# Half-width block inversion of a delta-rule mixer, its masked copies moved to GpSimd, and its norms moved to a later stage

## The chip, the cores and the metric

The program runs on one core of one Trainium2 chip. The metric is the device time of one execution in microseconds (us). The engines are named as in the profile: PE (TensorE, with PEld for its weight loads), DVE (VectorE), ACT (ScalarE), POOL (GpSimd) and SP (SyncE, which issues the DMAs).

## What is computed

The reference is two small transformer stacks in float32, one after the other, on 256 tokens of width 1024. The first has a block with an mLSTM and stick-breaking mixer, then a block with a gated delta-rule mixer; each block ends in a cross-attention on a memory of 256 tokens and a squared-ReLU feed-forward. The second has a block with two kinds of attention and one with a block attention, each followed by a gated feed-forward. The change touches the delta-rule mixer, which solves one unit lower triangular system for each head and chunk:

```
def gated_deltanet(q, k, v, beta, log_alpha):
...
    kk = jnp.einsum('nbhtd,nbhsd->nbhts', kc, kc)
    lower = jnp.where(strict, bc[..., :, None] * kk * decay, 0.0)
    eye = jnp.eye(L, dtype=f32)
    rhs = jnp.concatenate([vc * bc[..., None], kc * (bc * jnp.exp(g))[..., None]], axis=-1)
    sol = lax.linalg.triangular_solve(lower + eye, rhs, left_side=True, lower=True, unit_diagonal=True)
...
    _, o = lax.scan(step, S0, (u_c, w_c, attn, q_dec, k_dec, g_last))
    return _from_chunks(o)
```

The result of each head is normed over its 128 values and multiplied by a gain and by the SiLU of a gate. The kernel uses two chunks of 128 tokens in place of the reference's chunks of 64, which gives the same result.

## The kernel before

The weights are streamed from HBM as 458 panels of 128 x 1024 float32 (8 blocks of 128 x 128 each), in a fixed order, into a ring of six slots (`RING`). SP fetches panel n as soon as PE has counted panel n - 6 as used (L305 to L312). ACT rounds each panel to `ring_hi` (`reach`, L910 to L917), up to `LEAD` = 3 panels ahead of the stage that it serves, and POOL makes `ring_lo`, the rest, in two pieces of 128x512 for each panel (`low_part`, L321 to L327); `ring_lo` lies over the raw panel. The activations are split in the same way (`x_hi`, `x_lo`), and `project` and `project_tokens` (L379 and L421) form hi*hi + lo*hi + hi*lo on PE. All engines run their own instruction streams, written out in order in Python, and meet by semaphores. A `bank` of PSUM is taken in turn from four of ACT and four of DVE, and PE waits for what frees it.

The delta-rule stage of the first stack has eight heads, in two halves of four (`for half in range(2)`, PE L720, ACT L1157, DVE L1679). One half has eight 128 x 128 matrices: four heads by two chunks, in two groups `g` of four, each group one PSUM bank. In a half:

1. For each head, PE broadcasts the gate row (`gb`), DVE and ACT form the decays, PE the key and query products, and DVE writes `gd_at` (the strictly triangular matrix, transposed) and `gd_attn` (L1684 to L1699).
2. The inversion runs over seven levels (`LEVELS`). At level k, `cut(k, g)` (DVE, L1702) multiplies `gd_at` by a 0/1 mask that keeps the blocks that join neighbouring diagonal blocks of size 2^k, and writes `gd_b`. PE forms Y = B^T T (4 matmuls a group, ACT copies Y to `gd_y`), then the update of T (`gd_t`, not at the last level) and that of its transpose (`gd_tt`), 4 matmuls each; DVE subtracts them (`renew`, L1708). The matmuls are float32, and each one is two records in the trace.
3. A chain of small products for the four heads ends in the head outputs in `qkv4[:, 2]` and their squares in `sq`; two matmuls with a matrix of ones sum the squares (PE L796 to L798), and ACT computes the inverse root twice (`rsqrt`, L1200).

`mix_heads(0)` (DVE, L1671) takes these factors of the first half, norms the heads and multiplies by the gate; it stands in DVE's stream of the second half, after the first head of step 1 (L1681). ACT computes the SiLU of the whole gate (128x2048) in the first half, between steps 1 and 2 (L1181), with a table load before and after it.

After the second half, `memory_side` (PE L547, ACT L997) projects the memory into keys (four banks of two output tiles each, `xk1`) and values (four banks, `xv1`), 16 panels in all; DVE forms the memory's parts first (`mem_parts`), then `mix_heads(1)` and `mix_parts`, from which the mixer's output projection starts. POOL's stream holds nothing but `low_part`, in one loop over the ring (L329 to L334), so that it does nothing while no panel is used. Through the whole delta-rule stage no panel is used: the ring is full and all queues stand.

Of the kernel before, what the change touches and what calls it, by code (L numbers as in the profile page):

```python
# [45 lines left out]
P = 128  # L46
T = 256
# [85 lines left out]
def build_program(nc, panels, consts_in, smalls_in, x_in, mem_in, pos_in, out):  # L133
    with ExitStack() as ctx:
# [106 lines left out]
        gd_cols = area(16384, 8, 8)  # L241
        gd_row = lambda i: mixT[0:GD_H, (4 + i) % C, :]
# [77 lines left out]
        def _(pool):  # L320
# [8 lines left out]
            rounds = N_PANELS // RING  # L329
            with pool.Fori(0, rounds) as r:  # L330
                for s in range(RING):
                    low_part(s, r * RING + s)
            for n in range(rounds * RING, N_PANELS):
                low_part(n % RING, n)  # L334
# [7 lines left out]
        def _(pe):  # L342
# [377 lines left out]
            for half in range(2):  # L720
# [21 lines left out]
                for k in range(LEVELS):  # L742
                    y_at = {}
                    for g in range(2):
# [6 lines left out]
                        else:  # L751
                            o = bank("act", "y_ready")
                            for j in range(4):
                                mm(o[:, j * P:(j + 1) * P], gd_b[:, 4 * g + j, :], gd_t[:, 4 * g + j, :], True, True,
                                   "act" if j == 3 else None)
                            y_at[g] = told.seen["y_ready"]
                    for g in range(2 if k else 0):
                        pe.wait_ge(sem("y_ready"), y_at[g])
                        pe.wait_ge(sem("t_ready"), t_at[g])
                        if k < LEVELS - 1:  # L760
                            o = bank("dve", "t_ready")
                            for j in range(4):
                                mm(o[:, j * P:(j + 1) * P], gd_tt[:, 4 * g + j, :], gd_y[:, 4 * g + j, :], True, True,
                                   "dve" if j == 3 else None)
                        o = bank("dve", "t_ready")
                        for j in range(4):
                            mm(o[:, j * P:(j + 1) * P], gd_y[:, 4 * g + j, :], gd_tt[:, 4 * g + j, :], True, True,
# [120 lines left out]
        def _(act):  # L888
# [268 lines left out]
            for half in range(2):  # L1157
# [21 lines left out]
                if half == 0:  # L1179
                    settle()  # L1180
                    tell(act.activation(gate, gate, ACT.Silu), "gate_silu")  # L1181
                    log_exp()
# [10 lines left out]
                for hh in range(HALF):  # L1193
# [3 lines left out]
                    tell(act.activation(sq[:, 4 + hh, :], o[:, 0:T], ACT.Square), "osq")  # L1197
                if half:
                    told.more("mixed", 2)
                for g in range(2):  # L1200
                    rsqrt(2 * T, 1.0 / P)
            memory_side(1, 0, 4)
# [71 lines left out]
        def _(dve):  # L1274
# [395 lines left out]
            levels = const("levels_t").rearrange("p (k c) -> p k c", c=P)  # L1670
# [8 lines left out]
            for half in range(2):  # L1679
                for s in range(HALF + 1):  # L1680
                    if half and s == 2:  # L1681
                        told.more("gate_silu")
                        mix_heads(0)
# [18 lines left out]
                def cut(k, g):  # L1702

                    settle()
                    tell(dve.tensor_tensor(gd_b[:, 4 * g:4 * g + 4, :], gd_at[:, 4 * g:4 * g + 4, :],  # L1705
                                      spread(levels[:, k, :], 4), ALU.mult), "b_ready")

                def renew(m, g):  # L1708
                    o = take().rearrange("p (j b) -> p j b", b=P)
                    m = m[:, 4 * g:4 * g + 4, :]  # L1710
                    tell(dve.tensor_tensor(m, m, o, ALU.subtract), "t_ready")  # L1711

                for g in range(2):
                    cut(0, g)
                for g in range(2):
# [5 lines left out]
                    cut(1, g)  # L1721
                for k in range(1, LEVELS):
                    for g in range(2):
                        if k < LEVELS - 1:
                            renew(gd_t, g)
                            cut(k + 1, g)
# [222 lines left out]
```

## Time and profile before

| what | us |
| --- | --- |
| median of 3 runs | 1736.66 (1736.13 to 1749.96) |
| the profiled execution's own time | 1722.62 |
| its span | 1720.8 |
| busy in it: PE | 1603.2 (93%) |
| PE weight loads | 1514.6 (88%) |
| DVE | 796.1 (46%) |
| ACT | 808.1 (47%) |
| POOL | 1188.0 (69%) |

The span is what the profiler saw of one execution; the execution itself took 1.8 us more. The busy shares are means over the whole span, so they tell little of one stage: for that, the rows further down are taken from stretches of the trace, with their times counted from the start of the span. "PEclk" is the granted TensorE clock as a share of full speed. A row of a timeline gives the start, the duration of the merged instructions, their engine, line and operation, and in square brackets how long the engine sat idle before them and what ended that.

### The profile page before, as it was taken

To read this page: it belongs to the slowest core of one execution; us is meant where nothing else is said; L and a number is where in the kernel's file an instruction comes from. 1 tells how busy PE (TensorE), PEld (TensorE's weight loads), DVE (VectorE), ACT (ScalarE), POOL (GpSimd) and SP (SyncE) were. 2 spreads that over 40 slices of the span, in tenths; PEclk is the share of its full clock that TensorE was granted. 3 is DMA by queue.
4 is the path that set the end of the run, shared out by engine and by line. 5 is a ranking of instruction groups with operands and counts; after the bars stand their busy time and mean duration, and the time that the engine had idled before them with its cause. 6 is when DMAs were issued, how large, how long until landed. Compare 5 with 4: busy or idle time off the path is not lost.

```text
span 1720.8 us, 32818 instructions
## 1 busy us (share of the span) xinstructions
PE 1603.2 (93%) x12776; PEld 1514.6 (88%) x12776; DVE 796.1 (46%) x1430; ACT 808.1 (47%) x1169; POOL 1188.0 (69%) x920
## 2 busy tenths in 40 slices
PE   4979999999999987999999996989999999899997
PEld 3976998999988785999999995978999999799997
DVE  6038366320166465636532004655655335575523
ACT  3473544554455435444455442555555443644442
POOL 3733994899967600098589993653899988279995
PEclk7998999999999998999999998999999999999999
DMA  5421553565544300055355552432566654155552
GB/s 213 160 88 63 172 181 111 172 196 192 191 157 154 116 1 1 13 173 181 110 173 191 193 195 72 136 111 84 175 196 195 193 168 143 58 169 193 195 196 98
DMA packets 67086, 248.55 MB, mean 144 GB/s; under 512 B 7440, under 2 KB 7696, under 8 KB 66448
## 3 DMA queue, kind: packets, MB, share of 16 engines
q1 hardware_dynamic: 66960, 246.69, 43.8%
q8 instruction: 101, 1.65, 0.4%
q14 instruction: 25, 0.20, 0.0%
HBM read 245.62 MB, written 1.05 MB: 143 GB/s over the span
## 4 chain that ended last, share of the span: by engine, by line
PE 52%; DVE 7%; ACT 1%; issue 1%; DVEq 0%; ACTq 0%
PE ps_dve L361 42%; PE ps_act L361 10%; DVE x_lo L1378 1%; DVE x_hi L1375 1%; PE ps_act L372 1%; DVE xT L1370 1%; DVE work L1711 1%; ACT work L977 1%; DVE work L1409 0%; DVE sq L1363 0%; DVE work L1705 0%; ACT work L931 0%; DVE sq L1343 0%; DVE xT L1328 0%; DVE x_lo L1335 0%
## 5 line engine op out<-in xcount | busy, mean ns | idle before, releaser
L326 POOL TENSOR_TENSOR ring_lo<-ring,ring_hi 128x512 fp32r<-128x512 f32 x916 | 1187.8, 1335 | 511.5 <-ACT ring_hi L917 508.5
L917 ACT ACTIVATE ring_hi<-ring 128x1024 fp32r<-128x1024 f32 x458 | 465.8, 1052 | 193.3 <-DMA ring<-panels 190.9
L361 PE MATMUL ps_dve<-x_hi,ring_hi 128*128 128x256 f32 x1728 | 415.6, 281 | 17.6 <-DVE x_lo L1378 17.4
L361 PE MATMUL ps_dve<-x_lo,ring_hi 128*128 128x256 f32 x1728 | 412.9, 279 | 0.0
L361 PEld LDWEIGHTS ps_dve<-x_hi,ring_hi 128*128 128x128 f32 x1728 | 328.8, 190 | 23.2 <-DVE x_lo L1378 18.9
L361 PEld LDWEIGHTS ps_dve<-x_lo,ring_hi 128*128 128x128 f32 x1728 | 329.1, 190 | 0.2
L361 PE MATMUL ps_dve<-x_hi,ring_lo 128*128 128x256 f32 x1728 | 243.1, 278 | 0.0
L361 PE MATMUL ps_dve<-work_parts,ring_hi 128*128 128x256 f32 x1728 | 225.3, 276 | 0.0
L361 PEld LDWEIGHTS ps_dve<-x_hi,ring_lo 128*128 128x128 f32 x1728 | 219.1, 190 | 0.2 <-POOL ring_lo L326 0.2
L361 PEld LDWEIGHTS ps_dve<-work_parts,ring_hi 128*128 128x128 f32 x1728 | 211.8, 188 | 0.0
L1370 DVE TENSOR_TENSOR xT<-xT,ps_dve 128x512 f32<-128x512 f32 x40 | 27.5, 688 | 325.7 <-PE ps_dve L361 325.1
L361 PE MATMUL ps_dve<-work 128*128 128x128 f32 (+4 forms) x800 | 122.5, 325 | 13.4 <-DVE scratch L1688 5.7
L361 PE MATMUL ps_dve<-work_parts,ring_lo 128*128 128x256 f32 x864 | 132.7, 276 | 0.0
L361 PEld LDWEIGHTS ps_dve<-work 128*128 128x128 f32 (+1 forms) x800 | 101.0, 203 | 34.7 <-issue 19.8
L931 ACT ACTIVATE work<-ps_act 128x512 f32<-128x512 f32 (+2 forms) x122 | 64.4, 528 | 141.4 <-PE ps_act L361 136.1
L361 PE MATMUL ps_act<-x_hi,ring_hi 128*128 128x256 f32 x392 | 101.5, 296 | 24.6 <-DVE x_lo L1335 16.5
L361 PEld LDWEIGHTS ps_dve<-work_parts,ring_lo 128*128 128x128 f32 x864 | 113.8, 188 | 0.0
L361 PEld LDWEIGHTS ps_act<-x_hi,ring_hi 128*128 128x128 f32 x392 | 77.3, 197 | 28.6 <-DVE x_lo L1335 18.6
L939 ACT ACTIVATE sq<-xT 128x512 f32<-128x512 f32 x40 | 25.3, 633 | 158.1 <-DVE xT L1370 158.1
L361 PE MATMUL ps_act<-x_lo,ring_hi 128*128 128x256 f32 x392 | 97.9, 287 | 0.0
L361 PE MATMUL ps_dve<-mix_hi,ring_hi 128*128 128x256 f32 x384 | 93.3, 280 | 0.0
L361 PE MATMUL ps_dve<-mix_lo,ring_hi 128*128 128x256 f32 x384 | 92.5, 278 | 0.0
(232 smaller groups left out, 2199.0 us busy)
## 6 DMA issues: line engine op xcount, KB each, us to landing
ring<-panels SPq DMA_DIRECT2D x458, 512.0 KB, 3.4
consts<-constants SPq DMA_DIRECT2D x1, 2208.0 KB, 14.8
xT<-x_t SPq DMA_DIRECT2D x1, 1024.0 KB, 5.0
memn<-mem_t SPq DMA_DIRECT2D x1, 1024.0 KB, 18.9
out_t<-xT SPq DMA_DIRECT2D x1, 1024.0 KB, 3.9
smalls<-small_operands SPq DMA_DIRECT2D x1, 849.5 KB, 7.9
consts<-constants SPq DMA_DIRECT2D x1, 129.5 KB, 4.8
angle_i<-positions SPq DMA_DIRECT2D x1, 128.0 KB, 6.3
```

The source lines that it names most:

```text
L326: pool.tensor_tensor(ring_lo[:, s, cs], ring[:, s, cs], plain(ring_hi[:, s, cs]), ALU.subtract).then_inc(sem("lo_made"), 1)
L361: ins = pe.matmul(o, lhsT, rhs, start=start, stop=stop, skip_group_check=True)
L372: mark(pe.transpose(o, a, ident[0:a.shape[0], 0:a.shape[0]]), full)
L917: tell(act.activation(ring_hi[:, n % RING, :], ring[:, n % RING, :], ACT.Copy), "hi_made")
L931: tell(act.activation(dst, src, func, scale=scale), name)
L939: tell(act.activation(sq[:, c:c + 2, :], xT[:, c:c + 2, :], ACT.Square), "to_add" if c < 2 * added else "squared")
L977: ins = act.activation(b[:, n, 0:cols], b[:, n, 0:cols], ACT.Exp, bias=pair_max[s % 3][:, 4 + n:5 + n])
L1370: tell(dve.tensor_tensor(xT[:, c:c + 2, :], xT[:, c:c + 2, :], o, ALU.add), "resid")
L1375: ins = dve.tensor_scalar(x_hi[:, i, :], xT[:, i, :], gain[:, i:i + 1], None, ALU.mult)
L1378: ins = dve.scalar_tensor_tensor(x_lo[:, i, :], xT[:, i, :], gain[:, i:i + 1], plain(x_hi[:, i, :]), ALU.mult, ALU.subtract)
L1711: tell(dve.tensor_tensor(m, m, o, ALU.subtract), "t_ready")
```

## The change

Four things change together:

- The masked copies are made by POOL (`cut` in its stream, between two calls of `low_parts`: the panel loop is split at panel `FIRST["xk1"] + LEAD + 1`). For a level above 1 a copy waits for `y_ready` of the level before, which frees `gd_b`.
- Only half of the columns is computed at each level: B^T T for the even blocks of columns (`even`), the update of T likewise, and that of its transpose for the odd blocks. Matmuls have 64 columns in place of 128, `renew` and the copy of Y 256 elements in place of 512, and ACT writes zeros to the other half of `gd_y` with a second instruction.
- The norms of both halves move into `memory_side`: two sums of squares behind its bank 1, two behind bank 2. DVE does both `mix_heads` after `mem_parts`.
- ACT's SiLU of the gate is cut in four pieces of 128x512, behind levels 1 to 4 of the first half.

```diff
+            ahead = FIRST["xk1"] + LEAD + 1
+            low_parts(0, ahead)
+            for half in range(2):
+                told.more("attn", HALF)
+                if half:
+                    told.more("osq", HALF)
+                for g in range(2):
+                    cut(0, g)
+                for k in range(1, LEVELS):
+                    for g in range(2):
+                        pool.wait_ge(sem("t_ready" if k == 1 else "y_ready"),
...
+                        cut(k, g)
+            low_parts(ahead, N_PANELS)
...
+                            pe.wait_ge(sem("t_ready"), t_at[g] - (k > 1))
                             o = bank("act", "y_ready")
                             for j in range(4):
-                                mm(o[:, j * P:(j + 1) * P], gd_b[:, 4 * g + j, :], gd_t[:, 4 * g + j, :], True, True,
+                                js = slice(4 * g + j, 4 * g + j + 1)
+                                mm(o[:, j * 64:(j + 1) * 64], gd_b[:, 4 * g + j, :], even(gd_t[:, js, :], k), True, True,
                                    "act" if j == 3 else None)
...
-                for g in range(2):
-                    pe.wait_ge(sem("osq"), told.seen["osq"] - 2 + 2 * g)
-                    mm(bank("act", "norm_used"), ones, sq[:, 4 + 2 * g:6 + 2 * g, :], True, True, "act")
-                if half:
-                    memory_side()
+
+            def delta_norms(i):
+                for g in {1: (0, 1), 2: (2, 3)}.get(i, ()):
+                    pe.wait_ge(sem("osq"), osq_at + 2 * g + 2)
+                    mm(bank("act", "norm_used"), ones, sq[:, 2 * g:2 * g + 2, :], True, True, "act")
+            osq_at = told.seen["osq"] - GD_H
+            memory_side(delta_norms)
...
-                        copy_out(gd_y[:, 4 * g:4 * g + 4, :], name="y_ready")
+                        y = gd_y[:, 4 * g:4 * g + 4, :]
+                        act.activation(even(y, k), dense(take(), k), ACT.Copy)
+                        tell(act.activation(odd(y, k), dense(const("ones"), k), ACT.Copy, scale=0.0), "y_ready")
+                    if half == 0 and k <= 4:
+                        gs = gate[:, 2 * k - 2:2 * k, :]
+                        tell(act.activation(gs, gs, ACT.Silu), "gate_silu")
+                log_exp()
...
+            memory_side(1, 0, 2)
+            for g in range(4):
+                if g == 2:
+                    memory_side(1, 2, 3)
+                if g >= 2:
+                    told.more("mixed")
+                rsqrt(2 * T, 1.0 / P)
+            memory_side(1, 3, 4)
...
-                    if half and s == 2:
-                        told.more("gate_silu")
-                        mix_heads(0)
...
             mem_parts()
+            told.more("gate_silu", 4)
+            mix_heads(0)
             mix_heads(1)
```

The order of instructions on DVE, at the start of the second half. In the kernel before, from the first head's last product to the second head's (`work` holds the matrices, `rstd` the norm factors, `scratch` the decays):

```order
L1699 TENSOR_TENSOR work<-ps_dve,scratch 128x256
L1312 SCALAR_TENSOR_TENSOR ps_act<-ps_act,rstd 128x512 [waits rstd,attn,gate_silu]
L1313 SCALAR_TENSOR_TENSOR ps_act<-ps_act,rstd 128x512 [waits dve_step]
L1315 SCALAR_TENSOR_TENSOR rstd<-ps_act,rstd 128x512 [waits dve_step]
L1676 SCALAR_TENSOR_TENSOR work<-work,smalls,rstd 128x512 [waits norm_used]
L1677 TENSOR_TENSOR mixT<-work 128x512 [waits dve_step]
```

The same place in the changed kernel, up to the next head's first instruction:

```order
L1745 TENSOR_TENSOR work<-work,scratch 128x128
L1746 TENSOR_TENSOR work<-ps_dve,scratch 128x256
L1734 COPY scratch<-ps_dve 128x512 [waits dve_full,attn]
L1735 TENSOR_TENSOR scratch<-ps_dve,consts 128x256
L1742 TENSOR_TENSOR work<-ps_dve,scratch 128x256 [waits decays,dve_full,gb]
```

The five instructions of `mix_heads` (twice over, ten in all) are gone from between the heads; they stand behind `mem_parts` now.

ACT's order in the memory's key projection, before: `hi` copies of panels (L917), copies of the finished banks (L931), and one wait for `mixed` behind the last key bank.

```order
L931 ACTIVATE work<-ps_act 128x512 [waits act_full,hi_made]
L917 ACTIVATE ring_hi<-ring 128x1024 [waits panel_here1]
L917 ACTIVATE ring_hi<-ring 128x1024 [waits panel_here2]
L931 ACTIVATE work<-ps_act 128x512 [waits act_full,hi_made]
L917 ACTIVATE ring_hi<-ring 128x1024 [waits panel_here3,mixed]
```

The same place in the changed kernel, from the copy of bank 2 on (L963 makes `hi`, L977 copies a bank, L990 to L999 are one `rsqrt`):

```order
L977 ACTIVATE work<-ps_act 128x512 [waits act_full,hi_made]
L990 ACT_TABLE_LOAD [waits mixed]
L998 ACTIVATE rstd<-ps_act,consts 128x512 [waits act_full,mem_keys]
L999 ACTIVATE rstd<-rstd 128x512 [waits act_step]
L990 ACT_TABLE_LOAD [waits mixed]
L998 ACTIVATE rstd<-ps_act,consts 128x512 [waits act_full,rstd]
L999 ACTIVATE rstd<-rstd 128x512 [waits act_step]
L963 ACTIVATE ring_hi<-ring 128x1024 [waits panel_here1]
L963 ACTIVATE ring_hi<-ring 128x1024 [waits panel_here2]
L977 ACTIVATE work<-ps_act 128x512 [waits act_full,hi_made]
L963 ACTIVATE ring_hi<-ring 128x1024 [waits panel_here3,mixed]
```

Two `rsqrt`, each behind a wait for a `mixed` of DVE, stand between the copy of key bank 2 and the next `hi` copies of panels.

## Rows read from the trace of the kernel before

**Rows 1.** Timeline of PE in the inversion (first half; the last row, second half)

```profile
607.75 4.18 PE L361 MATMUL ps_act<-work 128*128 128x128 f32 x16 [1.48 <-DVE work L1705]
...
616.12 1.06 PE L361 MATMUL ps_act<-work 128*128 128x128 f32 x8
617.35 1.16 PE L361 MATMUL ps_act<-work 128*128 128x128 f32 x8 [0.17 <-DVE work L1705]
618.34 3.74 PE L361 MATMUL ps_dve<-work 128*128 128x128 f32 x32
621.92 1.06 PE L361 MATMUL ps_act<-work 128*128 128x128 f32 x8
...
687.61 2.26 PE L361 MATMUL ps_act<-work 128*128 128x128 f32 x16
```

**Rows 2.** Stretches: length; busy us of PE, PEld, DVE, ACT, POOL; clock, DMA, GB/s

```profile
607.00:613.00 6.00, 5.22 (x22) 4.92 (x23) 2.67 (x4) 3.39 (x4) 0.00 (x0) 0.50 0.02 4
620.00:630.00 10.00, 9.65 (x84) 9.28 (x83) 7.77 (x12) 1.79 (x3) 0.00 (x0) 1.00 0.00 0
1480.00:1500.00 20.00, 18.82 (x158) 15.73 (x155) 12.07 (x56) 14.64 (x36) 0.00 (x0) 1.00 0.00 1
```

**Rows 3.** Timeline of DVE around both starts of a half

```profile
592.55 0.69 DVE L1687 COPY scratch<-ps_dve 128x512 f32<-128x512 f32 x1
...
603.61 0.42 DVE L1699 TENSOR_TENSOR work<-ps_dve,scratch 128x256 f32<-128x256 f32 x1
...
655.45 0.69 DVE L1687 COPY scratch<-ps_dve 128x512 f32<-128x512 f32 x1 [11.05 <-PE ps_dve L361]
...
674.48 0.42 DVE L1699 TENSOR_TENSOR work<-ps_dve,scratch 128x256 f32<-128x256 f32 x1
```

**Rows 4.** Timeline of PE at the end of the first half and of the second

```profile
652.13 2.16 PE L361 MATMUL ps_act<-sq,consts 128*128 128x512 f32 x4
654.22 1.98 PE L361 MATMUL ps_dve<-mixT,consts 8*128 8x512 f32 x4
...
723.50 2.16 PE L361 MATMUL ps_act<-sq,consts 128*128 128x512 f32 x4
725.09 0.68 PE L361 MATMUL ps_act<-x_hi,ring_hi 128*128 128x256 f32 x1
```

**Rows 5.** Timeline of PE: float32 matmuls with 4 and 65 moving columns

```profile
1075.71 3.73 PE L361 MATMUL ps_dve<-smalls,sq 128*128 128x4 f32 x32
...
1161.09 1.45 PE L361 MATMUL ps_dve<-work 128*128 128x65 f32 x12
```

**Rows 6.** Timeline of ACT: copy of Y, copies of 256 elements, `rsqrt`, key banks

```profile
617.27 0.60 ACT L931 ACTIVATE work<-ps_act 128x512 f32<-128x512 f32 x1 [4.65 <-PE ps_act L361]
...
650.38 0.38 ACT L1196 ACTIVATE work<-ps_act 128x256 f32<-128x256 f32 x1 [0.39 <-PE ps_act L361]
650.66 0.38 ACT L1197 ACTIVATE sq<-ps_act 128x256 f32<-128x256 f32 x1
...
724.49 1.28 ACT L944 ACT_TABLE_LOAD   x1
...
727.16 1.28 ACT L944 ACT_TABLE_LOAD   x1
...
737.06 0.60 ACT L931 ACTIVATE work<-ps_act 128x512 f32<-128x512 f32 x1 [3.16 <-PE ps_act L361]
...
742.71 0.60 ACT L931 ACTIVATE work<-ps_act 128x512 f32<-128x512 f32 x1 [3.16 <-PE ps_act L361]
```

**Rows 7.** Lines by themselves: shortest, median and longest duration in ns

```profile
L1370 DVE TENSOR_TENSOR xT<-xT,ps_dve x40: 686/687/691, 215.8 to 1707.2; 128x512 f32<-128x512 f32 x40
...
L1677 DVE TENSOR_TENSOR mixT<-work x4: 691/692/1662, 664.0 to 734.0; 128x512 f32<-128x512 f32 x4
```

**Rows 8.** Timeline of POOL before the mixer, and from the memory stage on

```profile
459.37 18.87 POOL L326 TENSOR_TENSOR ring_lo<-ring,ring_hi 128x512 fp32r<-128x512 f32 x15
...
730.84 33.66 POOL L326 TENSOR_TENSOR ring_lo<-ring,ring_hi 128x512 fp32r<-128x512 f32 x24 [141.66 <-ACT ring_hi L917]
```

More of the change, by code:

```diff
@@ L327, in low_part, with low_parts, cut @@
                                        ALU.subtract).then_inc(sem("lo_made"), 1)
[L329 to L334, printed above, removed]
+            def low_parts(start, stop):
+                n = start
+                while n < stop and n % RING:
+                    low_part(n % RING, n)
+                    n += 1
+                rounds = (stop - n) // RING
+                if rounds:
+                    with pool.Fori(n // RING, n // RING + rounds) as r:
+                        for s in range(RING):
+                            low_part(s, r * RING + s)
+                for n in range(n + rounds * RING, stop):
+                    low_part(n % RING, n)
+            told = Counts(pool, sem)
+            levels = const("levels_t").rearrange("p (k c) -> p k c", c=P)
+            def cut(k, g):
+                mask = levels[:, k:k + 1, :].broadcast_to((P, 4, P))
+                pool.tensor_tensor(gd_b[:, 4 * g:4 * g + 4, :], gd_at[:, 4 * g:4 * g + 4, :], mask,
+                                   ALU.mult).then_inc(sem("b_ready"), 1)
+            ahead = FIRST["xk1"] + LEAD + 1
[9 more added lines that the diff above has]
+                        pool.wait_ge(sem("t_ready" if k == 1 else "y_ready"),
+                                     half * (2 + 2 * (2 * (LEVELS - 2) + 1)) + g + 1 if k == 1 else half * 2 * (LEVELS - 1) + 2 * (k - 2) + g + 1)
+                        cut(k, g)
+            low_parts(ahead, N_PANELS)
         hidden_from = {}
@@ L1178, in _ @@
                         tell(ins, "act_out")
[L1179 to L1182, printed above, removed]
                 for k in range(1, LEVELS):
                     for g in range(2):
-                        copy_out(gd_y[:, 4 * g:4 * g + 4, :], name="y_ready")
+                        y = gd_y[:, 4 * g:4 * g + 4, :]
[5 more added lines that the diff above has]
+                log_exp()
                 for hh in range(HALF):
@@ L1196, in _ @@
                     act.activation(qkv4[:, 2, h, :], o[:, 0:T], ACT.Copy)
[L1197 to L1202, printed above, removed]
+                    tell(act.activation(sq[:, h, :], o[:, 0:T], ACT.Square), "osq")
+            memory_side(1, 0, 2)
[6 more added lines that the diff above has]
+            memory_side(1, 3, 4)
             squares("c_out", C, 4)
@@ L1700, in _, with renew @@
                 dve.wait_ge(sem("attn"), half * HALF + HALF)
[L1702 to L1714, printed above, removed]
+                def renew(m, k):
+                    tell(dve.tensor_tensor(m, m, dense(take(), k), ALU.subtract), "t_ready")
                 for g in range(2):
@@ L1724, in _ @@
                         if k < LEVELS - 1:
-                            renew(gd_t, g)
-                            cut(k + 1, g)
-                        renew(gd_tt, g)
+                            renew(even(gd_t[:, 4 * g:4 * g + 4, :], k), k)
+                        renew(odd(gd_tt[:, 4 * g:4 * g + 4, :], k), k)
             mem_parts()
+            told.more("gate_silu", 4)
+            mix_heads(0)
             mix_heads(1)
```

16 lines of the change are left out of this document (11 added, 5 removed).

## The prediction, made before the changed kernel was run

> **What bounds the kernel now.** I read three views. The page's rows by slice show PE near full nearly everywhere, and a stretch in the middle where POOL and the DMA queues stand: POOL is idle for 141.66 us before its row at 730.84 [rows 8]. That is the delta-rule stage; nothing streams there, so a microsecond saved in it is one off the end, as long as the stages behind it, which are bound by PE, do not give it back. The timeline of PE shows what one level of the inversion costs: its first group starts at 616.12 and that of the next level at 621.92, 5.80 us later [rows 1]. In it stand 8 + 8 + 32 = 48 matmul records; the 32 take 3.74 us with the tail of the last one, and the next row starts 3.58 us after them, 0.112 us each. 48 of these are 5.4 us: PE is the bound of a level, and only about 0.35 us is waiting, on DVE's masked copy (0.17 us idle before 617.35 in PE's row) and around it. The table of stretches agrees: 9.65 of 10 us busy, clock 1.00, POOL 0.00 [rows 2].
>
> **Does half the width halve PE's time?** The rows say no. A float32 matmul with 65 moving columns and full weights comes 12 times in 1.45 us, and one with 4 columns 32 times in 3.73 us [rows 5]; less a tail of some 0.15 us that is 0.11 us a record, the same as with 128 columns. So it is the weights, 128 columns each time, that set the pace, and their number stays 48 a level. I cost the narrower matmuls at 0.113 us, no gain.
>
> The Trainium skill speaks on both sides here. "TensorE: Matmul & The Clock Gate", section "Back-to-back issue gap", gives a gap that falls with the moving columns (about 25 to 30 ns at 64); by that, doubled for the passes of float32, a record would need half of 0.11, which is the first rival below. The section on LDWEIGHTS in the same page lets the load go by the weight's columns, 107 ns for 128; this trace agrees with the latter (0.11 us at 4, 65 and 128 columns).
>
> **The change part by part**, against the span of 1720.8 us.
>
> *Levels 2 to 6.* ACT copies Y to two places: a PSUM copy of 256 elements starts 0.28 us before its successor and lasts 0.38 [rows 6], so the pair ends 0.66 us after its start, against 0.60 now; ACT starts 1.15 us after the group's first record (616.12 to 617.27) [rows 1, 6]. Y of group 0 is ready 1.81 us in, where PE's 16 records of the Ys also end (16 x 0.113), so about 0.1 us of waiting. The copies on POOL: the nearest row is its subtract of the same size, 15 in 18.87 us, 1.26 us each; the 24 from 730.84 on take 1.40 each [rows 8]. Two per level, started 1.9 and 3.2 us in, are there at 3.3 and 4.6, and PE wants them at 5.5 and 6.4. They are hidden by PE's 32 records; without that cover they would add up to 2 x 1.26. `renew` shrinks from 0.69 to about 0.42 us and is hidden anyway. A level becomes 5.55: 4 intervals a half x 0.25 = 1.0, and about 0.3 at the last `renew`, which PE awaits. For both halves -2.6.
>
> *The start of an inversion.* Here POOL is on the path. The first cut of each group, then the build of T on DVE (L1719, L1720), then the second cut stand in a row. First half: `attn` is complete at 603.61 + 0.42 = 604.03 [rows 3]; the cut ends at 605.4, DVE's build at 607.8, the second cut at 609.2, where PE has its first Y at 607.75 now [rows 1]. L1719 has two SBUF operands. Such a row, L1677, takes 0.69 us alone and 1.66 us beside POOL, while L1370, with one operand in PSUM, stays at 0.686 to 0.691 through all of its 40 calls [rows 7]; so I charge L1719 up to 0.97 us more and `renew` nothing. Group 1's Y then starts at 611.5, and the next level at 611.5 + 5 x 8 x 0.113 = 616.0, against 616.12 now. That it is not later is due to the clock: in 607 to 613 it stands at 0.50 [rows 2] (1.2 GHz; PE had been mostly idle before), and the first 16 records take 4.18 us with their gap [rows 1]. With 64 columns I keep 0.113 us at that clock too. The bounds are 0.113 and the 0.21 that 128 columns cost there; I take the lower, because at full clock nothing of the columns showed, and keep 3.5 us a half for the other end. Second half: `attn` at 674.90, the next level at 687.61, 12.7 us now; as the first half, 12.0. Together -0.8.
>
> The skill's page "SBUF — State Buffer" (the shared port pair) has DVE and GpSimd lock each other out for a whole instruction. By that rule the wait could be a full 1.26 us, 0.3 more per L1719; it would make the four of them 1.2 us dearer. The trace, with 0.97, is a little below it.
>
> *Between the halves.* Today PE does two sums of squares from 652.13, the next broadcast at 654.22 [rows 4], and DVE starts 1.23 us later at 655.45 [rows 3]. It then needs until 674.90, 19.45 us, because the ten instructions of `mix_heads(0)` stand between the heads; in the first half the same work took 592.55 to 604.03, 11.5 us. Now the broadcast goes at 652.1, DVE at 653.4, and it is done at 664.9: -10.0. ACT's two `rsqrt`, 2.67 us each [rows 6], leave too. Its `log_exp` load of 1.28 us behind level 6 falls into the time of PE's last 16 records and costs nothing. The four pieces of SiLU (about 0.6 us each, one load) fall into ACT's pauses, 4.65 us before the copy at 617.27; nothing.
>
> *The end of the second half.* The sums of squares leave from before the memory stage: 725.09 - 723.50 = -1.6 [rows 4].
>
> *The memory stage.* They come back here: 4 x 1.0 = +4.0, since PE is the bound (5.65 us a bank, 737.06 to 742.71) [rows 6]. And new waits come. With 0 at its start: bank 1 is done at 11.3, the sums at 13.3; ACT's two `rsqrt` give factors at 15.2 and 17.8. DVE needs for each of four parts 3 x 0.70 + 0.75 + 1.66 + gaps = 4.7 us beside POOL, so `norm_used` of the second comes at 22.1 and frees the bank of key bank 3, where PE has been ready since 20.9: 1.2 us. ACT waits for `mixed` (24.6) before its fourth `rsqrt`, which ends at 27.3; only then does it make `hi` of panels 9 and 10, so PE's value bank 0 starts 0.5 late (28.4 for 27.9) and waits about 0.8 on POOL's low part of panel 9. Then ACT waits for the last `mixed` at 34.0, and panel 11 is late by 0.3 and its low part by 0.8. Sum 3.6 us of stalls. POOL, at 1.40 us a piece just as fast as PE's 2.82 us a panel, loses its lead: +0.5. `mix_parts` ends at 46.7, before the output projection at about 53. Bounds of the stalls: 0, and 8 if the lead is not won back. Memory stage: +8.1.
>
> Sum: -2.6 - 0.8 - 10.0 - 1.6 + 8.1 = -6.9 us, a span of 1713.9. The profiled execution's own time would be 1715.7; the median of the runs shown lies 14.0 above that of before (1736.66 against 1722.62), so I predict 1729.8 as the median, 0.4% less.
>
> **The rivals.**
> 1. *Half width pays in full.* Then PE needs 24 x 0.113 = 2.7 us a level and the bound becomes the chain Y, copy, update, `renew`, with POOL's two copies: about 3.6 us. 10 intervals x 1.95 = 20 us more, and some 2 at the last levels: -29, 1708. For it: cycles fed to the array do halve. Against it: rows 5. Chance 0.10.
> 2. *The moved norms cost no stall*, since DVE is quicker than I have it (L1676 and L1677 not slowed), and the second half keeps its full clock: -6.9 - 4.1 - 2 = -13, 1724; its better half lies beyond 1%. Chance 0.22.
> 3. *The clock stays down (slower).* At 64 columns the array works half of the time, and if that does not lift the clock to 2.4 GHz, all 272 narrow records of a half run at it; it costs from the point at which a record needs over 0.13 us. At 0.21, the price of 128 columns there, 2 x 272 x 0.10 = +54, less the 6.9: +47, 1784. Against it: in 1480 to 1500, with many 65-column records, the clock is 1.00 [rows 2], and 4 columns for 3.7 us ran at 0.11 us. Chance 0.07.
> 4. *POOL does not keep up*, so the change does not do what it says: a copy with a repeated mask operand takes over 2.3 us; at 2.5 each level is about 0.7 longer, 10 x 0.95 = +9.5 against 5.55, +3 in all, 1740. Against it: all POOL rows of this size. Chance 0.07.
>
> **How the numbers follow.** My forecast has 0.54; its own range, from the bounds of the half-clock price (+7) and the stalls (-3.6 to +4.4), is 1724 to 1741. About 1% is what a measurement of this kernel can tell from no change, 17 us. Faster by more: rival 1 (0.10), half of rival 2 (0.11) and 0.03 of my own, 0.24. Slower by more: rival 3 (0.07) and 0.01. Within: 0.68. The range for 8 in 10 leaves out rival 3 and the better part of rival 1: 1710 to 1745.
>
> **What would show it.** PE's rows in the inversion: 48 records in some 5.4 us with 128x64 (right), or 2.7 (rival 1), or the clock at 0.50 beyond the first level (rival 3). POOL's copies near 1.26 us and no idle time of PE named after them from level 2 on. DVE without `mix_heads` between the heads, and 11.5 us from broadcast to last `attn`. PE's idle time in the memory stage, named after DVE (`norm_used`), ACT's `hi` and POOL's low part, 3 to 4 us. If a level is far from 5.55 or the memory stage from 53, I am wrong there.

## The result: slower by 2.8%, and the trace after

The changed kernel takes 1786.04 us (median, 1780.59 to 1800.19), beside 1743.31 us of the kernel before on the same chip: a ratio of 1.0279, interval 1.0232 to 1.0327 (the two medians alone give 1.0245, inside it). I had 1729.8 and a range up to 1745. The profiled execution took 1780.59 us; its span is 58.0 us longer than that of before (1778.8 against 1720.8).

The page of the changed kernel, its first two parts (busy time, then 40 slices of 44 us in tenths):

```profile
span 1778.8 us, 32742 instructions
PE 1661.7 (93%) x12776; PEld 1574.2 (89%) x12776; DVE 767.9 (43%) x1402; ACT 812.0 (46%) x1197; POOL 1224.0 (69%) x948
PE   4979999999999898999999998898999999899997
PEclk7998999999999757599999999898999999999999
```

PE looks as busy as ever. The row under it is the one to read: in slices 14 to 17, which are the delta-rule stage, the granted clock is 0.7, 0.5, 0.7, 0.5. The timeline of PE in the first inversion shows what one level costs now; it answers to [rows 1]:

```profile
614.71 1.97 PE L401 MATMUL ps_act<-work 128*128 128x64 f32 x8 [1.83 <-POOL work L358]
617.20 1.97 PE L401 MATMUL ps_act<-work 128*128 128x64 f32 x8 [0.53 <-POOL work L358]
618.96 7.03 PE L401 MATMUL ps_dve<-work 128*128 128x64 f32 x32
625.79 3.62 PE L401 MATMUL ps_act<-work 128*128 128x64 f32 x16
...
636.02 3.62 PE L401 MATMUL ps_act<-work 128*128 128x64 f32 x16
...
674.36 9.41 PE L401 MATMUL ps_act<-work 128*128 128x128 f32 x64 [0.58 <-DVE work L1750]
```

From one level to the next it is 10.24 us (625.79 to 636.02) where it was 5.80, with the same 48 records and no idle time: 0.213 us a record. The table of stretches has the clock beside it (length; busy us of PE, PEld, DVE, ACT, POOL; clock, DMA, GB/s), to be held against [rows 2]:

```profile
593.00:609.00 16.00, 15.93 (x37) 9.27 (x36) 8.52 (x23) 7.74 (x28) 0.00 (x0) 0.50 0.09 33
640.00:660.00 20.00, 20.00 (x96) 20.00 (x95) 3.37 (x8) 3.53 (x10) 4.62 (x5) 0.50 0.00 1
678.00:684.00 6.00, 5.98 (x50) 5.68 (x49) 0.00 (x0) 4.71 (x17) 0.00 (x0) 1.00 0.00 0
740.00:760.00 20.00, 19.42 (x92) 19.23 (x91) 3.52 (x9) 4.04 (x9) 2.54 (x2) 0.50 0.00 1
```

The clock is at its lower level, 1.2 GHz, in the attention part of the heads (593 to 609), comes up for a moment, falls during PE's pauses at the inversion's start (613) and stays down to the inversion's end. It is back at 2.4 GHz from 677 on, a few us after PE has begun on the 128-column products of the heads (674.36). The second half goes the same way. A PE that is busy for 20.00 of 20 us is not at its peak here; 96 records in 20 us against 84 in 9.65 us says it.

The other places of the prediction. DVE at the second half's start and in its two builds of T, which take as long in the first half (answers to [rows 3]), POOL's masked copies, and the waits of PE in the memory stage:

```profile
684.93 0.69 DVE L1734 COPY scratch<-ps_dve 128x512 f32<-128x512 f32 x1 [10.62 <-PE ps_dve L401]
...
694.67 0.42 DVE L1746 TENSOR_TENSOR work<-ps_dve,scratch 128x256 f32<-128x256 f32 x1
697.28 0.93 DVE L1756 TENSOR_TENSOR work<-consts,work 128x512 f32<-128x512 f32 x1 [2.19 <-PE ps_dve L412]
...
698.90 1.80 DVE L1756 TENSOR_TENSOR work<-consts,work 128x512 f32<-128x512 f32 x1
```

```profile
617.55 1.27 POOL L358 TENSOR_TENSOR work<-work,consts 128x512 f32<-128x512 f32 x1 [0.40 <-ACT work L1229]
```

```profile
789.92 0.38 PE L401 MATMUL ps_act<-x_hi,ring_hi 128*128 128x256 f32 x1 [0.52 <-DVE rstd L1366]
796.13 0.36 PE L401 MATMUL ps_act<-ring_hi,x_hi 128*128 128x256 f32 x1 [0.48 <-ACT ring_hi L963]
798.66 1.21 PE L401 MATMUL ps_act<-ring_lo,x_hi 128*128 128x256 f32 x8 [0.41 <-POOL ring_lo L336]
```

**Where the 58 us are**, after against before, each from the starts of the same rows in both timelines:

| part | us |
|---|---|
| heads of the first half, code as before: 17.1 for 11.5, clock 0.50 throughout | +5.6 |
| last head to the first Y, both halves | +2.4 |
| first Y to level 2, both halves (11.1 for 8.4 and 8.5) | +5.3 |
| four intervals of a level a half, 81.9 for 46.3 in both halves | +35.6 |
| level 6 and the wait for the heads' products, 7.6 for 5.15 a half | +4.9 |
| the heads' products, both halves, the first part of them at the lower clock | +3.1 |
| between the halves: DVE 10.2 us for 19.45, and the sums of squares | -11.4 |
| the second half's sums of squares | -1.6 |
| memory stage and output projection (what is left to the first residual row after them, 50.1 us later than before) | +6.2 |
| behind it, code as before | +7.9 |

The four rows from the first Y to the heads' products, +48.9 us, are nearly all time at the lower clock. The +2.4 ahead of them is not: PE waits there for POOL's copies and DVE's build (idle 2.06, 0.57 and 1.83 us, named after POOL), with the clock at 1.00 from 610 to 613. And the +5.6 of the heads is time at the lower clock, but not the change's: it lies ahead of the first changed instruction. The clock falls between 592 and 593 in both kernels; it is back by 597 in the kernel before, and not until 609 in the changed one. The profiled run of e5 further down, which has no narrow product at all, has the same stretch at 0.50 from 601 to 617, with PE busy 16.00 of 16 us. So this part is scatter between executions, and its cause is open.

The last row has no cause in the change that I can name, but the trace shows where most of it is. In the feed-forward stage PE does 172 records in 20 us in the changed kernel, 179 in the kernel before, at clock 1.00 in both. A stretch of it (length; PE busy; clock, DMA, GB/s), first of after, then of before:

```profile
940.00:960.00 20.00, 20.00 (x172) 1.00 0.55 185
```

```profile
940.00:960.00 20.00, 20.00 (x179) 1.00 0.62 198
```

### The profile page after: what moved, and what is told of

Same layout as the page of the kernel before. It is cut to its first block, busy times and chain, and to the rows that moved or that the text cites. A ratio compares the mean times of both kernels' runs of the same rounds, so it can differ in the third digit from the quotient of the medians.

```text
span 1778.8 us, 32742 instructions
## 1 busy us (share of the span) xinstructions
PE 1661.7 (93%) x12776; PEld 1574.2 (89%) x12776; DVE 767.9 (43%) x1402; ACT 812.0 (46%) x1197; POOL 1224.0 (69%) x948
## 4 chain that ended last, share of the span: by engine, by line
PE 79%; DVE 10%; issue 4%; POOL 3%; ACT 3%; DMA 0%; DVEq 0%; SPq 0%; POOLq 0%; ACTq 0%
PE ps_dve L401 64%; PE ps_act L401 14%; POOL ring_lo L336 3%; DVE x_lo L1429 2%; DVE x_hi L1426 1%; PE ps_act L412 1%; DVE xT L1421 1%; DVE sq L1414 1%; DVE work L1460 1%; DVE sq L1394 1%; ACT ring_hi L963 0%; DMA smalls<-small_operands 0%; ACT L990 0%; ACT work L977 0%; ACT work L1023 0%
## 5 line engine op out<-in xcount | busy, mean ns | idle before, releaser
L963 ACT ACTIVATE ring_hi<-ring 128x1024 fp32r<-128x1024 f32 x458 | 465.7, 1052 | 194.9 <-DMA ring<-panels 188.8
L401 PE MATMUL ps_dve<-work 128*128 128x64 f32 (+4 forms) x800 | 157.2, 386 | 10.9 <-ACT work L977 3.4
L401 PEld LDWEIGHTS ps_dve<-work 128*128 128x128 f32 (+1 forms) x800 | 135.5, 262 | 32.2 <-issue 13.4
L401 PE MATMUL ps_act<-x_hi,ring_hi 128*128 128x256 f32 x392 | 101.8, 297 | 25.5 <-DVE x_lo L1386 16.8
L358 POOL TENSOR_TENSOR work<-work,consts 128x512 f32<-128x512 f32 x28 | 35.5, 1271 | 121.6 <-ACT work L1229 64.8
L401 PE MATMUL ps_act<-work 128*128 128x64 f32 (+3 forms) x432 | 88.3, 381 | 12.7 <-ACT work L1139 6.4
L401 PEld LDWEIGHTS ps_act<-work 128*128 128x128 f32 (+1 forms) x432 | 79.4, 264 | 17.7 <-ACT work L1139 7.0
```

The lines of the kernel that those rows point to most:

```text
L358: pool.tensor_tensor(gd_b[:, 4 * g:4 * g + 4, :], gd_at[:, 4 * g:4 * g + 4, :], mask, ALU.mult).then_inc(sem("b_ready"), 1)
L401: ins = pe.matmul(o, lhsT, rhs, start=start, stop=stop, skip_group_check=True)
L963: tell(act.activation(ring_hi[:, n % RING, :], ring[:, n % RING, :], ACT.Copy), "hi_made")
```

## The experiments

Three theories. **A**: the narrow matmuls are the cause; while the clock is at 1.2 GHz, PE at 64 moving columns a record does not bring it back (form A1: it does hold a clock that is already up; form A2: it lets that fall too). **B**: it is POOL's copies, since PE waits longer at the start of an inversion. **C**: a 64-column record costs 0.213 us whatever the clock is, for instance by its strided reads.

**e1_full_width**: the changed kernel with whole rows of 128 columns in all products, and with them the one copy of Y and the full `renew`; POOL's copies, the moved norms and SiLU's pieces stay. In the cut, `W(k)` is 128 at every level and `even` returns the whole matrix:

```
-  mm(o[:, j * 64:(j + 1) * 64], gd_b[:, 4 * g + j, :], even(gd_t[:, js, :], k), ...
+  mm(o[:, j * W(k):(j + 1) * W(k)], gd_b[:, 4 * g + j, :], even(gd_t[:, js, :], k), ...
```

> The changed kernel with 128 moving columns at every level again (POOL's copies, the moved norms and the SiLU in pieces stay). Theory A (the narrow matmuls leave TensorE's clock at 1.2 GHz, and there a record costs 0.213 us): the clock comes back to 2.4 GHz within the first level, 48 records of a level take about 5.45 us, a level 5.4 to 5.8 us in place of 10.24, and the time is near the sum forecast without the clock's effect, some 5 to 10 us under the kernel before. Rival B (POOL's copies and the gaps at the start of the inversion hold the clock down, not the width): levels stay near 10 us, the time stays some 40 us over the kernel before.

Measured: ratio 0.9972, 0.9934 to 1.0009. PE's timeline:

```profile
615.64 2.08 PE L413 MATMUL ps_act<-work 128*128 128x128 f32 x8 [0.42 <-POOL work L370]
617.51 4.89 PE L413 MATMUL ps_dve<-work 128*128 128x128 f32 x32
622.23 1.95 PE L413 MATMUL ps_act<-work 128*128 128x128 f32 x16
624.04 3.84 PE L413 MATMUL ps_dve<-work 128*128 128x128 f32 x32
627.71 1.95 PE L413 MATMUL ps_act<-work 128*128 128x128 f32 x16
```

It starts with nearly the same pauses (1.38 and 0.42 us before the two Ys) at the lower clock (8 records in 2.08 us), and within level 1 the clock comes back: 4.89 us for 32 records, then 3.84. A level is 5.48 us. The whole loss is gone with nothing but the width and the sizes that follow from it changed, so B falls. The interval takes in 1: this run shows that the loss is gone, not that the rest of the change is a gain.

**e2_narrow_alone**: the kernel before with the 64-column products, ACT's two copies of Y and the smaller `renew` alone.

> The kernel before with the half-width matmuls, copies of Y and subtractions alone; the masked copies stay on DVE, the norms and the SiLU where they were. Theory A: clock 0.50 from the first level on, a record 0.213 us, a level 10.2 us, 45 to 55 us over the kernel before, and more than the changed kernel by what the moved norms save. Rival B: the clock returns as in the kernel before, a level 5.5 us, within 5 us of it.

Measured: ratio 1.0277, 1.0210 to 1.0344. The loss is there in full without POOL; that it would be larger than the changed kernel's by what the moved norms save does not show (1.0279). PE:

```profile
624.76 3.62 PE L370 MATMUL ps_act<-work 128*128 128x64 f32 x16
...
635.00 3.62 PE L370 MATMUL ps_act<-work 128*128 128x64 f32 x16
```

It is not the profiled executions alone: over the whole span the mean granted clock is 0.922 to 0.935 in all eight executions of the changed kernel and of e2, and 0.955 to 0.968 in those of the kernel before and of e1.

**e3_wide_first**: the changed kernel with 128 columns at levels 1 and 2, 64 from level 3 on.

> The changed kernel with 128 columns at levels 1 and 2 and 64 from level 3 on, so that the narrow matmuls start when the clock has come back. It tells two forms of theory A apart. A1 (64 columns hold a clock that is up, they only don't raise it): 0.113 us a record and 5.5 us a level from level 3 on, the whole some 5 to 10 us under the kernel before. A2 (64 columns let it fall): the clock falls to 0.50 within level 3 or 4 and the levels after it take 10.2 us, the whole 20 to 35 us over the kernel before. Rival B (POOL holds the clock down): 10 us already at levels 1 and 2.

Measured: ratio 0.9965, 0.9921 to 1.0009. PE, and the stretches with the clock:

```profile
631.19 1.90 PE L413 MATMUL ps_act<-work 128*128 128x64 f32 x16
633.03 3.79 PE L413 MATMUL ps_dve<-work 128*128 128x64 f32 x32
636.65 1.95 PE L413 MATMUL ps_act<-work 128*128 128x64 f32 x16
```

```profile
631.00:650.00 19.00, 19.00 (x168) 18.67 (x166) 6.00 (x14) 6.13 (x17) 7.51 (x6) 1.00 0.00 1
650.00:655.00 5.00, 4.42 (x29) 4.28 (x28) 0.84 (x2) 2.68 (x8) 0.00 (x0) 0.75 0.01 3
```

The same instructions with the same strided operands that took 10.24 us a level take 5.46 to 5.52 here. C falls: the price hangs on the clock. It is also the price of 128 columns, 5.48: at full clock half the width gives nothing, as [rows 5] had said. One sign of weakness is in the second stretch: the clock held through 168 narrow records and fell right behind them, at a pause of 0.58 us ahead of the heads' products. With wide levels a longer pause (0.85 us in the kernel before) left it up.

**e4_half_weights**: the changed kernel with 64 weight columns in the products of levels 1 to 6.

```
-  mm(o[:, j * 64:(j + 1) * 64], gd_b[:, 4 * g + j, :], ...
+  mm(o[0:64, j * 64:(j + 1) * 64], gd_b[:, 4 * g + j, 0:64], ...
```

> The changed kernel with only 64 of the 128 weight columns in every matmul of levels 1 to 6 (outputs of 64 partitions); it leaves out half of each product. It asks what sets 0.213 us at 64 moving columns and half clock. If the weight load sets it and goes with the clock (theory A): the clock stays at 0.50, a record costs about half, 0.107 to 0.13 us, and a level falls from 10.24 to 6 to 7 us, bounded by the chain of waits. If it is not the load but a fixed cost, or the strided reads of the 64 moving columns (rival C): the record stays at 0.21 us and the level at 10.2 us.

Measured: ratio 0.9782, 0.9724 to 0.9840 (two runs). PE:

```profile
614.36 1.12 PE L401 MATMUL ps_act<-work 128*64 128x64 f32 x8 [1.38 <-POOL work L358]
615.27 3.52 PE L401 MATMUL ps_dve<-work 128*64 128x64 f32 x32
...
622.02 1.35 PE L401 MATMUL ps_act<-work 128*64 128x64 f32 x16
623.49 2.08 PE L401 MATMUL ps_dve<-work 128*64 128x64 f32 x32
625.40 1.37 PE L401 MATMUL ps_act<-work 128*64 128x64 f32 x16
```

A level is 3.38 us; within a row a record takes 0.06 us, and at the lower clock the 8 records from 614.36 to 615.27 took 0.114 each. With 128 weight columns and the same 64 moving columns it was 0.113 and 0.213. So the number of weight columns sets the pace at both clocks, and the pace goes with the clock. I was wrong on one point: the clock did come back here, between 618 and 619, with 64 moving columns a record, and in the second half too. What sets this kernel's records apart from those of the changed kernel is that they follow each other in half the time. So the theory has to be held to what the runs showed: 64 moving columns together with 128 weight columns did not bring the clock back.

**e7_wide_one and e10_narrow_fillers** ask how much it takes. The first has 128 columns at level 1 alone. The second has 64 at all levels, and products of constants with 128 columns, which feed nothing, in PE's pauses at the inversion's start:

```
+  o = bank("act", "y_ready")
+  for _ in range(8 if (k, g) == (1, 0) else 0):
+      mm(o[:, 0:P], ident, ident, True, True)
```

> The changed kernel with 128 columns at level 1 alone and 64 from level 2 on. With 128 columns at levels 1 and 2 the clock stood at 1.00 all through the narrow levels; with 64 at all levels it stood at 0.50 to the end. If it is enough that the clock has come back before the narrow levels begin, this hangs on whether level 1 does it: in the full-width run the clock rose at about 619 to 620, within level 1, whose 48 records end at 622, so I expect a level of 5.5 us from level 2 on, and a ratio of 0.995 to 1.000. Rival: the rise comes too late in some halves, one half runs at 0.50 with 10.24 us a level (+18 to 20 us), ratio about 1.01; both halves, 1.02 or above.

Measured: ratio 1.0009, 0.9967 to 1.0052, just above what I expected, with 1 well inside. PE in the first half, levels 2 and 3:

```profile
616.70 1.90 PE L413 MATMUL ps_act<-work 128*128 128x64 f32 x16
...
622.16 1.95 PE L413 MATMUL ps_act<-work 128*128 128x64 f32 x16
```

Level 1 was enough here, in both halves: from level 2 on it is 5.5 us a level. In the second half the clock fell behind the last level, as in e3.

> The changed kernel, 64 columns at all levels, with matmuls of 128 columns that feed nothing put into PE's pauses at an inversion's start (5 before the transposes, 8 before the first Y). In the full-width kernel such fillers had the clock at 1.00 from about 609 on, 8 us before level 1's updates. If 64 columns hold a clock that is up and only fail to bring it back, the narrow levels take 5.5 us each here and the ratio is 0.995 to 1.000 instead of 1.028. Rival: the narrow levels pull the clock down wherever they come early, since nothing of 128 columns stands within the inversion; then levels of 10.24 us come back and the ratio stays above 1.02.

Measured: ratio 1.0219 (1.0010 to 1.0428, two runs); the profiled run has one half of either kind, and the other execution, 1781.95 us, had a mean clock of 0.934 over its span, as low as the changed kernel. PE at the second Y of the first half, then stretches of the first half and, last, of the second:

```profile
620.14 1.08 PE L401 MATMUL ps_act<-work 128*128 128x64 f32 x8 [1.44 <-POOL work L358]
```

```profile
612.00:617.00 5.00, 2.82 (x25) 2.42 (x23) 2.71 (x5) 1.13 (x4) 3.22 (x3) 1.00 0.00 0
617.00:621.00 4.00, 2.56 (x22) 2.27 (x21) 1.69 (x2) 0.71 (x2) 2.77 (x3) 1.00 0.00 0
621.00:627.00 6.00, 6.00 (x31) 6.00 (x30) 1.27 (x3) 2.62 (x4) 1.54 (x2) 0.51 0.02 4
630.00:670.00 40.00, 40.00 (x189) 40.00 (x189) 6.74 (x16) 6.85 (x19) 10.22 (x8) 0.50 0.00 0
703.00:735.00 32.00, 31.85 (x277) 31.19 (x275) 8.87 (x22) 9.54 (x25) 13.81 (x11) 1.00 0.00 1
```

In the first half the clock was up while the fillers ran, PE then paused 1.44 us before the second Y, and the clock fell with the first narrow updates (0.51 from 621). It stayed down for the other levels, 40 us of PE without a pause. In the second half it had fallen before the second set of fillers (0.50 from 700 to 703), was up again at 703 behind them, and PE went on into the narrow levels without a pause; all of them ran at 1.00. So neither answer that I had written down holds for both halves: the narrow levels kept a clock that was up where no pause stood among them, and a clock once lost to a pause they did not get back. Over all profiled halves with 64 columns and full weights: a clock that was down did not come back in 5 of 5 (after, e2, e10's first); one that was up stayed up through the levels in 5 of 5 (e3, e7, e10's second). That a pause before the levels is what decides rests on e10's two halves alone.

**e5_norms_alone, e6_pool_alone**: the kernel before with one of the two other parts each.

> The kernel of before with one part of the change alone: the sums of squares and the two gated mixes of the delta-rule stage stand in the memory stage; the inversion, its masked copies on DVE and the one SiLU are those of before. By my first working: between the halves -10.0 us, end of the second half -1.6, memory stage +4.0 for the sums and 0 to 3.6 of stalls, so -7.6 to -4.0 us against before, a ratio of 0.9956 to 0.9977. The profile of the changed kernel showed stalls of 1.4 us only in the memory stage, so I now lean to the lower end, 0.996. Rival: the memory stage gives it all back through POOL's lost lead, ratio 1.000 or above. In the profile: DVE's stretch between the halves near 10 us instead of 19.45.

Measured: ratio 0.9944, 0.9900 to 0.9987. DVE between the halves:

```profile
667.74 0.69 DVE L1689 COPY scratch<-ps_dve 128x512 f32<-128x512 f32 x1 [9.05 <-PE ps_dve L361]
...
677.49 0.42 DVE L1701 TENSOR_TENSOR work<-ps_dve,scratch 128x256 f32<-128x256 f32 x1
```

667.74 to 677.91 is 10.2 us in place of 19.45, as expected. The part is a gain, a small one: the interval ends at 0.9987.

> The kernel of before with the masked copies of the levels on POOL alone, full width, with norms and SiLU as before. A level was 5.80 us with the copies on DVE and 5.48 with them on POOL (the run with full width of the changed kernel): 8 intervals x 0.32 = -2.6 us; the start of each inversion has POOL's copies of 1.27 us in the chain in place of DVE's of 0.7, 2 x (2 x 0.6 + up to 1.1 of DVE beside POOL) = +2.4 to +4.6. Sum 0 to +2 us, a ratio of 1.000 to 1.001. Rival: POOL's copies are what made the full-width version faster than before, ratio 0.997.

Measured: ratio 0.9962, 0.9932 to 0.9992, better than the 1.000 to 1.001 I expected. A level is 5.48 us here too. The two starts are 2.2 us longer than before (13.1 and 13.9 us from the last `attn` to level 2, against 12.1 and 12.7), a little under what I had. And there is a step that I had not counted: level 6 takes 4.70 us in place of 5.15, -0.9 for both halves. From the first head to the memory stage the profiled run is 1.1 us shorter than before (131.4 against 132.5), which would be 0.9993, beside the interval's upper end of 0.9992. So the trace has about one microsecond of gain, and what the median has beyond it is not explained.

e5 and e6 together are what e1 has beside the old inversion; their product is 0.9906 and e1's ratio is 0.9972. The intervals are too wide to say which is nearer, so the size of either gain is not settled.

**e8_last_quarter**, the version that came out of these: 128 columns at levels 1 to 5, and at level 6, where the parts that aren't zero are one half of the partitions, 64 weight columns too.

```
+  mm(o[64:P, j * 64:(j + 1) * 64], gd_b[:, 4 * g + j, 64:P], gd_t[:, 4 * g + j, 0:64], ...
+  mm(o[0:64, j * 64:(j + 1) * 64], gd_y[:, 4 * g + j, 0:64], gd_tt[:, 4 * g + j, 64:P], ...
```

> The changed kernel with 128 columns at levels 1 to 5, and at level 6 64 weight columns and 64 moving columns for both products, since there the blocks that are not zero lie in one half of the partitions; its output is the same. The half-weight run had 0.06 us a record at full clock against 0.113, so 32 records of level 6 are 1.7 us a half less; the chain from Y over ACT to the update takes part of it back. I expect 1.0 to 1.7 us a half less than with full width, 2 to 3.4 in all, so a ratio of 0.995 to 0.997 against before (full width had 0.9972). Rival: the last level is bound by its chain through ACT and DVE, and nothing is gained, 0.997.

Measured: 1721.41 us, ratio 0.9888, 0.9834 to 0.9942: 1.1% under the kernel before, and with that under the changed one. Its last level:

```profile
641.84 1.14 PE L413 MATMUL ps_act<-work 128*64 128x64 f32 x16
...
644.31 0.68 PE L413 MATMUL ps_dve<-work 128*64 128x64 f32 x8 [0.16 <-ACT work L1253]
645.57 7.84 PE L413 MATMUL ps_act<-work 128*128 128x128 f32 x64 [0.58 <-DVE work L1790]
```

From 641.84 to the heads' products at 645.57 it is 3.73 us. In e6, with full weights, it is 4.70 (639.38 to 644.08), of which 0.27 is the longer wait behind the larger `renew` (0.85 for 0.58). So it is about 1 us a half. That and e1 make 0.9960; the rest of the way to 0.9888 I can't name from the change (6 runs, whose interval reaches to 0.9942; the last section has a source of scatter that may hold it).

**e9_fillers**: e8 with fillers of 128 columns, 5 before the transposes and 3 before the first Y.

> The kernel with the short last level, and in the two pauses of PE at an inversion's start (2.6 us before the transposes, 1.4 us before the first Y) 5 and 3 matmuls of 128 weight columns and 128 moving columns whose result is written over. If what brings the clock back is PE streaming 128 columns a record for a while, it is at 1.00 from about 617 instead of 620 and some 25 records cost 0.1 us less each: 2 to 3 us a half, a ratio 0.002 to 0.003 under the kernel without them, so 0.992 to 0.995. Rival: the fillers end after POOL is ready and only delay (up to +0.5 us a half), ratio 0.996 to 0.998, with the clock up at the same time as before.

Measured: ratio 0.9942, 0.9908 to 0.9976: not better than without. In the trace the fillers have the clock at 1.00 when the first Y starts:

```profile
607.46 1.53 PE L413 MATMUL ps_dve<-consts 128*128 128x128 f32 x10
...
613.45 1.16 PE L413 MATMUL ps_act<-work 128*128 128x128 f32 x8 [1.10 <-POOL work L370]
615.99 1.13 PE L413 MATMUL ps_act<-work 128*128 128x128 f32 x8 [1.38 <-POOL work L370]
```

The first Y take 1.16 us in place of 2.08. But POOL's copies are what comes last there, so the pause grows by as much (1.38 before the second Y, 0.41 before). From the last transposes of the heads to level 2 it is 13.9 us (606.61 to 620.53) against 14.9 in e8, one microsecond a half. That is too little to be seen beside the scatter, and the ratio doesn't show it.

## Why the prediction was wrong

The step that failed is the price of a narrow record, 0.113 us at every place of an inversion, and it failed in two terms.

The greater is "Levels 2 to 6": "A level becomes 5.55" took over the clock of 1.00 in [rows 2], which stands there under 128-column products, for products of 64 columns, without a reason. The runs showed the clock at 0.50 to the end of the inversion, 0.213 us a record and 10.24 us a level. The four intervals and the last level of both halves came to +40.5 us in place of -2.6. That the clock would not come back was rival 3, and I gave it 0.07. The evidence against it was weak on two counts. The stretch at 1480 with its 65-column records had the clock up already and held other matmuls of up to 256 columns; and e3 shows that holding is another question than coming back. The 32 records with 4 columns took 0.11 us each, and the clock was up there too (1.00 from 1072 on, before the first of them). Neither row showed a clock that rises under narrow matmuls. With nothing in the trace that shows it, I would now give rival 3 some 0.3, and the range its time; that is a judgement, not a result.

The other is in "The start of an inversion": "With 64 columns I keep 0.113 us at that clock too. The bounds are 0.113 and the 0.21 that 128 columns cost there; I take the lower, because at full clock nothing of the columns showed". That was no reason. At full clock the weights set the pace; e4 shows that the weights' pace goes with the clock, so at 1.2 GHz it is 0.213 us, with 64 moving columns as with 128. The row for it was in [rows 1]: 16 records in 4.18 us, with their gap, at clock 0.50. I had the right cause for the pace (weights) and didn't ask what it does at the other clock.

Rival 3 had the mechanism right. That its "1784" is so near to the 1786 measured is in part luck: its +47 was counted from 1736.66, while the kernel before took 1743.31 in this comparison, and the 58.0 us between the profiled executions hold 5.6 and 7.9 us for which I can name no cause in the change.

Point by point:
- *Half width gives nothing at full clock*: right. 5.46 to 5.52 with 64 columns (e3), 5.48 with 128 (e1); forecast 5.55. Rival 1 is out.
- *Levels 2 to 6, -2.6*: +40.5. Where the clock is up it is about right: e7, with these levels narrow, has 22.0 us for the four intervals of a half (23.2 and 23.1 before) and 4.48 us for level 6 (5.15 before), -3.6 in all.
- *The start of an inversion, -0.8*: +7.6. The first Y comes 5.1 us after the last `attn`, as I had it (5.2; 3.7 and 4.2 before), which is +2.4; from there to level 2 it is 11.1 us where I had 6.8. With level 1 wide (e7) the starts take 13.0 and 12.7 us, against 12.1 and 12.7 before and the 12.0 that I had.
- *Between the halves, -10.0*: -11.4 (DVE 10.2 us, not 11.5: the waits for PE in the first half that I took it from, 0.97 and 0.51 us, are not there).
- *POOL's copies at 1.26, hidden from level 2 on*: right, 1.27. Rival 4 is out. *DVE's build beside POOL up to 1.66*: 0.93 and 1.80, so the bound was too low by 0.14, and `renew` with its PSUM operand unaffected at 0.42.
- *Memory stage +8.1*: +6.2. The sums cost 2 x 1.9. I had 3.6 us of stalls and 0.5 for POOL's lost lead; the rows are the 0.52, 0.48 and 0.41 shown above and two more on POOL's low part, 0.62 and 0.35 (at 805 and 811), 2.4 in all. I had the first of them right by its releaser (DVE's factors) and too large. With it rival 2, no stall at all, is out.
- *The end of the second half, -1.6*: right.

Without the failed step the rest fits: the parts other than the width make 0.9972 (e1, 0.9934 to 1.0009), and I had 0.996. So small a gain can't be told from none by that run.

The Trainium skill's "TensorE: Matmul & The Clock Gate", in its section on LDWEIGHTS, gives 107 ns for a load of 128 columns without naming the clock. The 0.113 us of [rows 1] agree, the 0.213 us of the lower clock do not; the measurement decides. Its section on the clock gate says that sustained matmul activity releases the throttle. Here narrow matmuls that stood one behind the other from 617 to 674 did not release it: the clock was at 0.50 throughout.

## What to carry to other kernels

Before you make matmuls narrower, look in which state of the clock that stretch begins: if PE comes to it from pauses, keep the first level wide (here one level of 48 records with 128 columns was enough, e7), and read the granted clock, not PE's busy time, to see what you got. Where each matmul loads its own weights, going from 128 to 64 moving columns saved nothing here (0.113 us a record for both at full clock); going from 128 to 64 weight columns did (0.06). For a price at the lower clock take a row at the lower clock.

## What the runs showed that I had not expected

- PE can be busy for 55 us on end at 1.2 GHz. With 64 moving and 128 weight columns (float32) it stayed there in 5 halves of 5; with 64 and 64 (e4), and with 128 and 128, it was back within the first level or right behind it in every half. Narrow products are not the only place for it: the heads of the first half, whose code is the same everywhere, had PE busy at 0.50 for 16 us in the changed kernel and in e5, 13 in e1, and 3 in the kernel before.
- The clock fell behind narrow levels at a pause of 0.58 us in 2 of 5 halves (e3, first half: 1.00 up to 652, 0.50 at 653; e7, second half: 0.50 at 702), where wide levels left it up at 0.85 us in the kernel before.
- Four feed-forward stages of some 160 us, whose code is the same in every kernel here, ran each at one of two paces, 172 or 179 records in 20 us, with the clock at 1.00 in both. Which stage had which changed from one profiled execution to the next: none of four at 172 in the kernel before and in e8, one in after, e2, e4, e5, e6, e7 and e10, two in e1, e3 and e9. It is 4%, 6 to 7 us a stage, so up to 26 us over all four, and the kernel before scattered over 25.5 us in 19 executions (1725.5 to 1751). The cause is open. It also means that effects under 0.5% are hardly settled by these runs.
